# DeltaNet's triangular inverse: levels 1 to 5 on diagonal blocks of 64 rows, four chunks written out

## What is computed

```python
gamma = jnp.exp(jnp.where(tril, gc[..., :, None] - gc[..., None, :], -jnp.inf))
kb = k * beta[..., None]
low = jnp.where(strict, jnp.einsum('bhncd,bhnsd->bhncs', kb, k) * gamma, 0.0)
rhs = jnp.concatenate([v * beta[..., None], kb * jnp.exp(gc)[..., None]], axis=-1)
sol = lax.linalg.triangular_solve(jnp.eye(c, dtype=low.dtype) + low, rhs,
                                  left_side=True, lower=True)
u, w = sol[..., :dv], sol[..., dv:]
attn = jnp.einsum('bhncd,bhnsd->bhncs', q, k) * gamma
...
def step(s, xs):
    u_c, w_c, attn_c, qd_c, kd_c, gl_c = xs
    v_new = u_c - jnp.einsum('bhcd,bhde->bhce', w_c, s)
    o = jnp.einsum('bhcd,bhde->bhce', qd_c, s) + jnp.einsum('bhcs,bhse->bhce', attn_c, v_new)
    s = s * jnp.exp(gl_c)[..., None, None] + jnp.einsum('bhcd,bhce->bhde', kd_c, v_new)
    return s, o
```

## Time and profile before

| | us |
|---|---|
| median of 3 runs | 1858.63 (1847.7 to 3455.2) |
| the profiled execution's time | 1854.68 |
| its span | 1853.0 |
| the four prompt chunks of DeltaNet | 201.5 |
| of one chunk, the seven levels and what prepares them (from the first matmul of the last `kq` to the second group's `wt`) | 29.4 |

### The profile page before, as it was taken

The page is one execution under the profiler, slowest core; times in us unless marked ns, Lnnn a source line. Parts: engine busy times, 40 slices in busy tenths (PEclk is TensorE's granted clock), DMA queues, the critical chain, the costliest instruction groups (busy, mean ns, idle before and its releaser), DMA issues. The chain is left out here.

```text
span 1853.0 us, 36268 instructions
## 1 busy us (share of the span) xinstructions
PE 1760.0 (95%) x13404; PEld 1636.5 (88%) x13404; DVE 1012.1 (55%) x1848; ACT 722.0 (39%) x1239; POOL 403.2 (22%) x580
## 2 busy tenths in 40 slices
PE   8999899999799999999999999799899999999997
PEld 6999788888598999999999998555598999999997
DVE  4763455551528766767225433576537666678224
ACT  4343333331536333335224311556446333336222
POOL 1554344453001222221000000343300222221000
PEclk9999999998899999999999999899999999999999
DMA  4222211100521222223222224889721222222322
GB/s 174 79 79 80 71 35 35 34 20 1 193 80 57 87 83 79 79 85 102 91 91 69 80 68 156 290 290 326 256 84 54 84 85 79 79 82 75 101 90 86
DMA packets 78367, 188.61 MB, mean 102 GB/s; under 512 B 9442, under 2 KB 25186, under 8 KB 77906
## 3 DMA queue, kind: packets, MB, share of 16 engines
q1 hardware_dynamic: 71618, 168.47, 26.8%
q0 software_dynamic: 6672, 19.10, 3.1%
HBM read 176.00 MB, written 11.55 MB: 101 GB/s over the span
## 5 line engine op out<-in xcount | busy, mean ns | idle before, releaser
L674 PE MATMUL PB<-parts,wparts 128*128 128x288 f32 x8664 | 1170.2, 297 | 21.9 <-DVE wparts L643 10.9
L674 PEld LDWEIGHTS PB<-parts,wparts 128*128 128x128 f32 x8664 | 1164.6, 190 | 26.1 <-DVE wparts L643 21.1
L633 ACT ACTIVATE wparts<-ring 128x1024 fp32r<-128x1024 f32 x198 | 209.8, 1059 | 684.8 <-PE PB L674 683.9
L643 DVE TENSOR_TENSOR wparts<-ring,wparts 128x1024 fp32r<-128x1024 f32 x174 | 212.8, 1224 | 274.3 <-ACT wparts L633 264.7
L1033 POOL COPY cnew<-arena 128x2 f32 (+1 forms) x106 | 115.1, 1085 | 344.0 <-DVE arena L958 341.2
L970 DVE SCALAR_TENSOR_TENSOR arena<-arena,ffw 128x512 f32<-128x512 f32 x176 | 133.7, 760 | 19.4 <-DVE arena L971 12.8
L955 DVE TENSOR_TENSOR arena<-PB,stats 128x288 f32<-128x288 f32 x88 | 40.2, 457 | 127.8 <-PE PB L674 121.2
L684 PE MATMUL PB<-parts,wparts 128*128 128x288 f32 x648 | 104.7, 310 | 3.9 <-DVE parts L513 3.3
L684 PEld LDWEIGHTS PB<-parts,wparts 128*128 128x128 f32 x648 | 91.0, 188 | 12.9 <-DVE parts L513 7.3
L1009 DVE SCALAR_TENSOR_TENSOR arena<-arena,dnw 128x512 f32<-128x512 f32 x54 | 58.0, 1075 | 32.8 <-ACT arena L908 27.6
L932 ACT ACTIVATE arena<-arena,ffw 128x512 f32<-128x512 f32 x88 | 63.8, 725 | 27.0 <-issue 15.5
(11 more groups left out here) (299 smaller groups left out, 2091.8 us busy)
## 6 DMA issues: line engine op xcount, KB each, us to landing
ring<-in_w SPq DMA_DIRECT2D x198, 512.0 KB, 3.2
arena<-in_kpages SPq DMA_DIRECT2D x64, 256.0 KB, 5.5
arena<-in_vpages SPq DMA_DIRECT2D x64, 256.0 KB, 5.2
arena<-in_kpages POOLq DMA_DIRECT2D x64, 128.0 KB, 2.8
arena<-in_vpages POOLq DMA_DIRECT2D x64, 128.0 KB, 5.0
membuf<-in_w SPq DMA_DIRECT2D x8, 512.0 KB, 5.7
arena<-in_state_dn SPq DMA_DIRECT2D x6, 512.0 KB, 5.0
o_dns_s<-arena SPq DMA_DIRECT2D x6, 512.0 KB, 3.9
```

Of the source, the lines that this page charges most:

```text
L633: nc.scalar.activation(wparts[:, 0, k, :], ring[:, k, :], ACT.Copy).then_inc(hi_ready, 1)
L643: nc.vector.tensor_tensor(wparts[:, 1, k, :], ring[:, k, :], wparts[:, 0, k, :].bitcast(F32), ALU.subtract).then_inc(lo_ready, 1)
L674: last = nc.tensor.matmul(dst(b), wparts[:, part, k, block * P:(block + 1) * P], x[:, row_, b * HALF:(b + 1) * HALF], start=start and part ...
```

## The change

The two 64-row blocks on the diagonal of each head's matrix are kept side by side in 64 columns, [128, heads, 64] instead of [128, heads, 128]: rows 0 to 63 hold the first block, rows 64 to 127 the second. Levels 0 to 5 never leave these blocks, so they work on this packed form alone. A matmul of a head becomes two of 64x64, one on array rows and columns 0 to 63, one on 64 to 127, whose results land in the two halves of the partitions of the same PSUM bank. Tm and TT of a group lie side by side in one tile (`TXb`), and the results x and xt in one bank, so one subtraction on DVE updates both. Level 6 stays as it was, on full 128x128 tiles that DVE fills from the packed form (`em`, `et`). Level 0 is made on DVE (two operations and a transpose of 32x32 blocks), without POOL, PE and ACT. `lb`, the full product with beta, is needed for level 6 alone and is moved behind level 1; its 64-column part (`lc`) takes its old place. The four chunks are written out instead of looped.

The packed views over the full tiles, and the packed form of a bank:

```diff
+        LTb = Tm.rearrange("p h n -> p (h n)")[:, 0:384].rearrange("p (h n) -> p h n", h=DN_H)
+        M1b = [Tm.rearrange("p h n -> p (h n)")[:, 384 + 192 * g:576 + 192 * g].rearrange("p (x h n) -> p x h n", x=1, h=3)
+               for g in range(2)]
+        BTb = TT.rearrange("p h n -> p (h n)").rearrange("p (l h n) -> p l h n", l=2, h=DN_H)
+        TXb = [M1.rearrange("p h n -> p (h n)")[:, 384 * g:384 * g + 384].rearrange("p (x h n) -> p x h n", x=2, h=3)
+               for g in range(2)]
...
+        def bank_b(b, T=P, x=0):
+            return PB[0:T, b, 192 * x:192 * x + 192].rearrange("p (h n) -> p h n", h=3)
```

In `dn_pe`:

```diff
             def vt(g):
                 wait("pool", "vst")
-                wait("dve", f"lb{g}")
+                wait("dve", f"lc{g}" if sample else f"lb{g}")
...
-            def t0(g):
-                wait("dve", f"tt0{g}")
+            def blocks(out, left, right):
                 for h in range(3):
-                    last = nc.tensor.transpose(bank(2 * g, T, T)[:, h, :], TT[0:T, 3 * g + h, 0:T], ident[0:T, 0:T])
-                last.then_inc(S_, mark(f"t0{g}"))
-            for step, g in ((kk, 0), (kq, 0), (kk, 1), (kt, 0), (kt, 1), (kq, 1), (vt, 0), (t0, 0), (vt, 1), (t0, 1)):
+                    for i in range(T // 64):
+                        b = slice(64 * i, 64 * i + 64)
+                        last = nc.tensor.matmul(out[b, h, :], left[b, h, :], right[b, h, :], start=True, stop=True)
+                return last
+
+            for step, g in ((kk, 0), (kq, 0), (kk, 1), (kt, 0), (kt, 1), (kq, 1)):
                 step(g)
             for l in range(1, levels):
-                if l > 1:
-                    wait("pool", f"bt{l}")
+                if l <= 5:
+                    for g in G:
+                        wait("pool", f"bt1_{g}" if l == 1 else f"bt{l}")
+                        wait("dve", f"tt0{g}" if l == 1 else f"x{l - 1}_{g}")
+                        blocks(bank_b(2 * g, T), BTb[0:T, (l - 1) % 2, 3 * g:3 * g + 3, :], TXb[g][0:T, 0, :, :]).then_inc(S_, mark(f"m{l}_{g}"))
+                    for g in G:
+                        wait("act", f"m{l}_{g}")
+                        if l == 1:
+                            wait("dve", f"at{g}")
+                        if l < levels - 1:
+                            blocks(bank_b(2 * g + 1, T), TXb[g][0:T, 1, :, :], M1b[g][0:T, 0, :, :])
+                        blocks(bank_b(2 * g + 1, T, 1), M1b[g][0:T, 0, :, :], TXb[g][0:T, 1, :, :]).then_inc(S_, mark(f"x{l}_{g}"))
+                    if l == 1:
+                        vt(0)
+                        vt(1)
+                    continue
+                wait("pool", f"bt{l}")
                 for g in G:
...
+                    wait("dve", f"em{g}")
...
                 for g in G:
                     wait("act", f"m{l}_{g}")
-                    wait("dve", f"at{g}" if l == 1 else f"xt{l - 1}_{g}")
+                    wait("dve", f"et{g}")
+                    wait("dve", f"vb{g}")
```

In `dn_act`:

```diff
-                    nc.scalar.activation(heads(M1, g, T, T), bank(g, T, T), ACT.Copy).then_inc(S_, mark(f"m{l}_{g}"))
+                    if l == 6:
+                        wait("dve", f"et{g}")
+                    if l <= 5:
+                        dst, src = M1b[g][0:T, 0, :, :], bank_b(2 * g, T)
+                    else:
+                        dst, src = heads(M1, g, T, T), bank(2 * g, T, T)
+                    nc.scalar.activation(dst, src, ACT.Copy).then_inc(S_, mark(f"m{l}_{g}"))
```

In `dn_dve`:

```diff
+            def lc(g):
                 wait("pe", f"bb{g}")
                 wait("dve", f"lt{g}")
+                for i in range(T // 64):
+                    b = slice(64 * i, 64 * i + 64)
+                    last = nc.vector.tensor_tensor(LTb[b, 3 * g:3 * g + 3, :], heads(LT, g, T, T)[b, :, b],
+                                                   bank(4 + g, T, T)[b, :, b], ALU.mult)
+                last.then_inc(S_, mark(f"lc{g}"))
+
+            def lb(g):
+                wait("dve", f"lc{g}")
                 nc.vector.tensor_tensor(heads(LT, g, T, T), heads(LT, g, T, T), bank(4 + g, T, T), ALU.mult).then_inc(S_, mark(f"lb{g}"))
 
             def tt0(g):
-                wait("pool", f"bt0_{g}")
-                nc.vector.tensor_tensor(heads(TT, g, T, T), ident[0:T, 0:T].unsqueeze(1).to_broadcast([T, 3, T]),
-                                        heads(M1, g, T, T), ALU.subtract).then_inc(S_, mark(f"tt0{g}"))
+                wait("dve", f"lc{g}")
+                tx = TXb[g][0:T, :, :, :]
+                nc.vector.tensor_tensor(tx[:, 1, :, :], heads_b(LTb, g, T), small_m[0:T, 0, :].unsqueeze(1).to_broadcast([T, 3, 64]),
+                                        ALU.mult).then_inc(dv.sem, dv.inc())
+                dve.wait_ge(dv.sem, dv.value)
+                nc.vector.tensor_tensor(tx[:, 1, :, :], tx[:, 1, :, :], small_m[0:T, 6, :].unsqueeze(1).to_broadcast([T, 3, 64]),
+                                        ALU.add).then_inc(dv.sem, dv.inc())
+                dve.wait_ge(dv.sem, dv.value)
+                nc.vector.transpose(tx[:, 0, :, :].rearrange("p h n -> p (h n)"),
+                                    tx[:, 1, :, :].rearrange("p h n -> p (h n)")).then_inc(S_, mark(f"tt0{g}"))
+
+            def full(name, dst, x, g):
+                wait("dve", f"x{5 if not sample else levels - 1}_{g}")
+                n = T // 64
+                nc.vector.tensor_tensor(heads(dst, g, T, T).rearrange("p h (j n) -> p h j n", j=n),
+                                        TXb[g][0:T, x, :, :].unsqueeze(2).to_broadcast([T, 3, n, 64]),
+                                        block2[0:T, 0:T].rearrange("p (j n) -> p j n", j=n).unsqueeze(1).to_broadcast([T, 3, n, 64]),
+                                        ALU.mult).then_inc(S_, mark(f"{name}{g}"))
...
-            for step, g in ((kn_, 0), (qn_, 0), (kn_, 1), (lt, 0), (lb, 0), (qn_, 1), (lt, 1), (lb, 1), (tt0, 0), (tt0, 1),
-                            (vb_, 0), (at, 0), (vb_, 1), (at, 1)):
+            for step, g in ((kn_, 0), (qn_, 0), (kn_, 1), (lt, 0), (lc, 0), (qn_, 1), (lt, 1), (lc, 1), (tt0, 0), (tt0, 1),
+                            (at, 0), (at, 1)):
                 step(g)
             for l in range(1, levels):
                 for g in G:
+                    if l <= 5:
+                        x0 = int(l == levels - 1)
+                        tx = TXb[g][0:T, x0:, :, :]
+                        wait("pe", f"x{l}_{g}")
+                        wait("dve", f"tt0{g}" if l == 1 else f"x{l - 1}_{g}")
+                        nc.vector.tensor_tensor(tx, tx, PB[0:T, 2 * g + 1, 192 * x0:384].rearrange("p (x h n) -> p x h n", x=2 - x0, h=3),
+                                                ALU.subtract).then_inc(S_, mark(f"x{l}_{g}"))
+                        continue
...
-                if l <= 2:
+                if sample:
+                    vb_(l - 1)
                     kd(l - 1)
+                elif l == 1:
+                    lb(0)
+                    lb(1)
+                elif l == 2:
+                    vb_(0)
+                    vb_(1)
+                elif l in (3, 4):
+                    kd(l - 3)
+                elif l == 5:
+                    for g in G:
+                        full("em", Tm, 0, g)
+                        full("et", TT, 1, g)
+            if sample:
+                for g in G:
+                    full("et", TT, 1, g)
```

In `dn_pool` and `dn_run`:

```diff
-            for l in range(2):
-                for g in G:
-                    wait("dve", f"lb{g}")
-                    nc.gpsimd.tensor_tensor(heads((M1, BT)[l], g, T, T), heads(LT, g, T, T),
-                                            levelm[l][0:T, 0:T].unsqueeze(1).to_broadcast([T, 3, T]),
-                                            ALU.mult).then_inc(S_, mark(f"bt{l}_{g}"))
-            for l in range(2, levels):
-                wait("pe", f"m{l - 1}_1")
+            for g in G:
+                wait("dve", f"lc{g}")
+                nc.gpsimd.tensor_tensor(BTb[0:T, 0, 3 * g:3 * g + 3, :], heads_b(LTb, g, T),
+                                        small_m[0:T, 1, :].unsqueeze(1).to_broadcast([T, 3, 64]), ALU.mult).then_inc(S_, mark(f"bt1_{g}"))
+            for l in range(2, min(levels, 6)):
+                if l >= 3:
+                    wait("pe", f"m{l - 2}_1")
+                nc.gpsimd.tensor_tensor(BTb[0:T, (l - 1) % 2, :, :], LTb[0:T, :, :],
+                                        small_m[0:T, l, :].unsqueeze(1).to_broadcast([T, DN_H, 64]), ALU.mult).then_inc(S_, mark(f"bt{l}"))
+            if not sample:
+                wait("dve", "lb1")
                 nc.gpsimd.tensor_tensor(BT[0:T, :, 0:T], LT[0:T, :, 0:T],
-                                        levelm[l][0:T, 0:T].unsqueeze(1).to_broadcast([T, DN_H, T]),
-                                        ALU.mult).then_inc(S_, mark(f"bt{l}"))
+                                        levelm[6][0:T, 0:T].unsqueeze(1).to_broadcast([T, DN_H, T]), ALU.mult).then_inc(S_, mark("bt6"))
...
```

(22 more changed lines are left out.)

61 lines of the change are left out of this document (31 added, 30 removed).

## The result

The changed kernel takes 1863.65 us (median of 20 runs, 1856.74 to 1869.49) where the kernel before takes 1857.36 in the same comparison: a ratio of 1.0043, 95% interval 1.0028 to 1.0057. The forecast was 1844. It missed the sign: the time grew by 6 us instead of falling by 11.

The account below looks back on a forecast made before the run. PE's work was taken to bound the kernel. 1854.7 - 17.2 (three chunks) - 0.9 (fourth) + 3 (sample part) + 5 (clock) = 1844 us; forecast case 1834 to 1856, range 1822 to 1870.

Parts of the forecast that it names:

- the forecast's sum for the stage: Whole DeltaNet stage, four chunks and sample part together: 10.4 us shorter.
- the second rival: Packed levels: the two array halves do not overlap, +2.4 us per chunk, 1868 us in all; chance 0.10.
- The halves overlap: Packed matmuls on opposite 64-row halves run fully side by side: 0.35 us for an `m` of a group, 0.51 with tail.
- The path was the forecast one: Levels 2 to 5: second group's path sets a 2.56 us period; second `wt` starts 5.75 us earlier per chunk.
- Writing the loops out, put at 0: Border of two chunks: PE shows no gap, so nothing gained, at most 0.15 us each.
- The clock: the step with the wrong size: Around level 1's `m`: granted clock falls to 0.50 once per chunk for 3.40 us, costing 1.2 each, +5 in all.
- The fourth chunk: Level 6 fills each wait for one POOL scaling of 1.87 us; chain grows some 4.9, leaving a gain of 0.9.
- The sample part: the step that failed: Sample part: some eight more operations of 0.36 us ahead of PE's work, no PE gain; +3, bounds 0 and 6.
- POOL's lock was priced as one operation at a time: DVE operations with two SBUF inputs lose to POOL; in the fourth chunk each fill waits for one operation of 1.87 us.

## Why the prediction was wrong

Between the forecast's sum for the stage and the measured one lie 19.8 us: 8.0 in the sample part, 3.6 in the fourth chunk, 8.2 in the other three. The measured 1863.65 lies in the interval that the second rival was given (1862 to 1872), but by accident, since that rival's mechanism is not there. (Its own sum is 1 too high: 8 less 5.75 is 2.25, not 2.4, which gives 1867.)

**Right, as to mechanism.** The halves overlap: 0.56 for an `m` with its tail, where 0.51 was taken. The Trainium skill ("TensorEngine Tiling (Array Packing)", "Gotcha 1: PSUM Pressure") says that different row tiles cannot access the same PSUM bank simultaneously. Here both halves write one bank, in different partitions, and 12 records take 0.56, where 6 on one quarter take 0.51 and 12 take 0.86; the measurement decides, and the second rival falls. At full clock (with three matmuls ahead of level 1) level 2 starts 8.75 behind the last `kq` (8.53 forecast), level 6 20.68 (19.83), the second `wt` 24.63 (23.63). The path was the forecast one, with a period of 2.70 where 2.56 was reckoned: the gain is 4.75 instead of 5.75. Writing the loops out, put at 0 since PE shows no gap at a chunk's border, made three chunks 0.5 to 0.6 us shorter in the run of its own; the saving lay inside the levels.

**The clock: the step with the wrong size.** "I expect one fall per chunk" was right; 1.2 us each was not. The fall was taken to last 3.40 us, as in the one row that showed one; behind the gap ahead of level 1 it lasted 6.83 to 10.24 in this execution, and cost 2.1 to 2.5 in the second and third chunk (48.18 and 47.71 against 45.73 and 45.61). The length is in part chance: the first chunk had 10.24 us there, and 2.9 more at its start, and took 49.79; the runs with the late scaling and with the old sample part, in which nothing of that chunk is changed, had 3.41 us in all and took 46.83 and 46.85. So the size of the shortest fall was taken for that of all.

**The fourth chunk.** The term had the right cause and was near in the fills (6.23 us, less 4 x 0.47, is 4.4 where 4.9 was said). But the late `m6` left PE idle twice (2.08 and 3.34 us), and level 6 then ran at half clock too. Mending the wait alone gave 6.3.

**The sample part: the step that failed.** "Bounds 0 and 6; I take +3": the upper bound was too low. It counted operations of 0.36 and left out two things that the prediction itself had named elsewhere. POOL's lock was priced as one operation at a time, yet DVE's add waited through four POOL operations on end, 4.38 us. And the clock was counted per chunk only: the longer chain with PE idle put the levels and the memory unit at 0.50, worth 3.9 us up to that unit's end. `et`, counted among the operations of 0.36, was worth 2.4 in the one trace without it.

The rule of the Trainium skill that stands behind that wait ("SBUF — State Buffer", "Who interferes with whom") calls the port pair that DVE and GpSimd share an exclusive lock. The 4.38 against 0.35 agrees with it.

## What to carry to other kernels

A gapless engine that is given less work becomes an engine with gaps, and here the gaps took back about half of what a chunk had saved (2.1 to 2.5 of 4.75 us): look which idle stretches a faster step opens ahead of dense work, and what the granted clock does behind each, before the gain is counted. A wait that another engine's operations bring can last for one of them, as in the fourth chunk, or for the whole run that stands in that engine's queue, as in the sample part: price both. Two executions of the same code can differ by some microseconds in the clock alone, so a small gain is to be read close to the place that was changed. And a packed form that pays where a block is half empty (128 rows) has nothing to give where the matrix is already 64 wide; that case should keep its old code.

## What was not expected of the hardware

- One DVE operation with two SBUF inputs was held for 4.38 us by consecutive POOL operations, in all four traces that have that order; where only the first two of these POOL operations stood there, it took 0.62, getting in between them. Why it did not get in between the same two when more followed stays open: no run here tells it.
- Matmuls on opposite quarters of the array overlap also where they don't alternate: three blocks of one quarter and then three of the other took 0.70, where 12 records on one quarter take 0.86, so the second three began before the first were through.
- PE's unused matmuls were worth more than they cost: 2.10 us of work in PE's idle time ahead of level 1 made a chunk 2.1 to 2.5 us shorter.
